# Three layer norms of a two-layer trunk kernel: tiles normalised directly, and the start and the query copies reordered

## The reference, cut to what matters

```python
for layer in range(DEPTH):                      # DEPTH = 2
    mix = _even_mixer(...) if layer % 2 == 0 else _odd_mixer(...)
    x = _layer_norm(ALPHA * x + mix, ln1_g[layer], ln1_b[layer])
    x = _layer_norm(ALPHA * x + _swiglu(x, ...), ln2_g[layer], ln2_b[layer])

def _layer_norm(x, g, b):
    mu = jnp.mean(x, -1, keepdims=True)
    xc = x - mu
    var = jnp.mean(xc * xc, -1, keepdims=True)
    return xc * lax.rsqrt(var + LN_EPS) * g + b
```

## Time and profile before

| what | value |
|---|---|
| median of 3 runs | 1243.77 us (1243.36 to 1244.42) |
| the profiled execution | 1243.55 us, its span 1241.7 us |
| PE busy | 1227.7 us, 99% of the span |
| DVE, ACT, POOL busy | 436.9, 450.6, 587.9 us |
| granted PE clock, mean | 0.998 of 2.4 GHz |
| DMA | 122.96 MB, mean 99 GB/s |

### The profile page before, as it was taken

One profiled execution on the slowest core, in us unless ns is written; L12 is line 12 of the kernel. 1 busy time (PEld: TensorE's weight loads), 2 busy tenths in 40 slices (PEclk: granted clock), 3 DMA queues, 4 the chain that ended last, 5 costly groups with the idle time before them and its releaser, 6 DMA issues.

```text
span 1241.7 us, 17153 instructions
## 1 busy us (share of the span) xinstructions
PE 1227.7 (99%) x7112; PEld 1012.4 (82%) x7112; DVE 436.9 (35%) x772; ACT 450.6 (36%) x670; POOL 587.9 (47%) x280
## 2 busy tenths in 40 slices
PE   9999999999999999999999999999999999999997
PEld 7878887888888888887777889888788888888885
DVE  4556526201011100127678845654511111110105
ACT  4167825232223221225544455542532233221211
POOL 4244444943444343445744347444684444435341
PEclk9999999999999999999999999999999999999999
DMA  9321052333322333232353342124233222324231
GB/s 321 96 69 69 3 169 69 102 102 102 99 93 80 98 124 118 102 102 60 92 123 116 91 114 94 27 69 136 68 102 102 92 92 88 102 85 146 75 102 68
DMA packets 106064, 122.96 MB, mean 99 GB/s; under 512 B 18946, under 2 KB 80580, under 8 KB 105988
## 3 DMA queue, kind: packets, MB, share of 16 engines
q1 hardware_dynamic: 98244, 118.56, 29.9%
q10 hardware_dynamic: 7744, 3.32, 1.1%
HBM read 117.93 MB, written 3.70 MB: 98 GB/s over the span
## 4 chain that ended last, share of the span: by engine, by line
PE 95%; DVE 3%; DVEq 0%; ACT 0%; issue 0%; ACTq 0%
PE bank L1665 27%; PE bank L1666 27%; PE bank L1667 27%; PE bank L2088 4%; PE bank L1696 1%; PE bank L1697 1%; PE bank L1709 1%; DVE stats L1239 1%; DVE x_tm L1237 1%; PE bank L1919 1%; PE bank L2197 1%; PE bank L1731 1%; PE bank L2034 1%; PE bank L2180 0%; PE bank L1855 0%; DVE x_tm L1200 0%
## 5 line engine op out<-in xcount | busy, mean ns | idle before, releaser
L681 POOL TENSOR_TENSOR w_lo<-w_raw,w_hi 128x1024 fp32r<-128x1024 f32 (+1 forms) x200 | 470.2, 2373 | 546.9 <-ACT w_hi L816 521.8
L1665 PE MATMUL bank<-x_hi,w_hi 128*128 128x512 f32 x880 | 344.3, 391 | 0.0
L1666 PE MATMUL bank<-x_lo,w_hi 128*128 128x512 f32 x880 | 342.5, 389 | 0.0
L1667 PE MATMUL bank<-x_hi,w_lo 128*128 128x512 f32 x880 | 342.5, 389 | 0.0
L816 ACT ACTIVATE w_hi<-w_raw 128x1024 fp32r<-128x1024 f32 (+1 forms) x200 | 196.4, 1032 | 206.5 <-issue 161.2
L1665 PEld LDWEIGHTS bank<-x_hi,w_hi 128*128 128x128 f32 x880 | 165.2, 188 | 35.4 <-issue 0.8
L1667 PEld LDWEIGHTS bank<-x_hi,w_lo 128*128 128x128 f32 x880 | 165.2, 188 | 34.4
L1666 PEld LDWEIGHTS bank<-x_lo,w_hi 128*128 128x128 f32 x880 | 165.2, 188 | 33.7
L1246 DVE TENSOR_TENSOR f_ab<-bank,f_ab 128x512 f32<-128x512 f32 x44 | 30.4, 692 | 364.7 <-PE bank L1667 364.7
L1667 PE MATMUL bank<-w_hi,h_lo 128*128 128x512 f32 x352 | 136.9, 389 | 0.0
L1665 PE MATMUL bank<-w_hi,h_hi 128*128 128x512 f32 x352 | 136.9, 389 | 0.0
(11 more groups left out here) (291 smaller groups left out, 1252.1 us busy)
## 6 DMA issues: line engine op xcount, KB each, us to landing
w_raw<-ffn_w_gate_dram SPq DMA_DIRECT2D x22, 1024.0 KB, 5.3
w_raw<-ffn_w_up_dram SPq DMA_DIRECT2D x22, 1024.0 KB, 5.3
w_raw<-ffn_w_down_dram SPq DMA_DIRECT2D x20, 1024.0 KB, 5.0
w_raw<-od_w_in_dram SPq DMA_DIRECT2D x16, 1024.0 KB, 5.8
w_raw<-ev_w_in_dram SPq DMA_DIRECT2D x8, 1024.0 KB, 5.6
w_raw<-ev_w_out_dram SPq DMA_DIRECT2D x4, 1024.0 KB, 5.1
w_raw<-od_w_out_dram SPq DMA_DIRECT2D x4, 1024.0 KB, 5.1
x_fm<-x_fm_dram SPq DMA_DIRECT2D x8, 256.0 KB, 6.9
```

Of the source, the lines that this page charges most:

```text
L681: pool.tensor_tensor(w_lo[:, b % 2, c], w_raw[:, b % 2, c], w_hi[:, b % 2, c].bitcast(F32), ALU.subtract).then_inc(w_lo_ready, 1)
L1665: pe.matmul(out_ap, st[0], mv_[0], start=start, stop=False)
L1666: pe.matmul(out_ap, st[0], mv_[1], start=False, stop=False)
L1667: return pe.matmul(out_ap, st[1], mv_[0], start=False, stop=stop)
```

## The change

Four edits in one.

In norms 1 to 3 DVE normalises each tile directly behind its own statistics. ACT rounds the first half of the next weight block ahead of the last tile's square root, and the second half behind `round_x`. With `round_x(2)` now ahead of them, the three DMAs of ACT in norm 2 are issued after it.

At the start 12 warm-up matmuls are run instead of 16; PE starts "sq" with four matmuls of high parts only, and then takes the other two products of column block 0.

ACT copies two tiles of queries and keys before it rounds the second "gv" block.

```diff
+            def split_part(b, j):
+                assert split[0] == b
+                if j == 0:
+                    act.wait_ge(w_landed[b % 2], 16 * (b // 2 + b % 2))
+                    act.wait_ge(*block_end[b - 2])
+                    low_weights_all(act, b - 2)
+                act.activation(w_hi[:, b % 2, pieces(b)[j]], w_raw[:, b % 2, pieces(b)[j]], ACT.Copy).then_inc(w_hi_ready, 1)
+                split[0] += j
+
-            def round_x(i):
+            def round_x(i, b):
...
+                split_part(b, 1)
+
-            def layer_norm(i):
+            def layer_norm(i, b=None):
                 for t in range(NT):
+                    if t == NT - 1 and b is not None:
+                        split_part(b, 0)
                     act.wait_ge(s["ln_var"], NT * (i - 1) + t + 1)
...
-            split_to(first_block[("gv",)] + 1)
             for t in range(NT):
+                if t == 2:
+                    split_to(first_block[("gv",)] + 1)
                 full(act, ("qT", t))
...
-            layer_norm(1)
-            split_to(first_block[("gate", 0, 0)] + 1)
-            round_x(1)
+            layer_norm(1, first_block[("gate", 0, 0)] + 1)
+            round_x(1, first_block[("gate", 0, 0)] + 1)
...
-            layer_norm(2)
-            split_to(first_block[("conv", KD)] + 1)
+            layer_norm(2, first_block[("conv", KD)] + 1)
+            round_x(2, first_block[("conv", KD)] + 1)
             act.dma_start(ba_w[:, :, :], ...)
...
-            round_x(2)
...
                             dve.bn_aggr(mv[:, t, :], ...).then_inc(s["ln_var"], 1)
-                            if i == 4:
-                                normalise(t)
-                            elif t:
-                                normalise(t - 1)
-                if i < 4:
-                    normalise(NT - 1)
+                            normalise(t)
...
-            for _ in range(16):
+            for _ in range(12):
                 pe.matmul(bank(("skv", NT - 1))[:, :], warm[:, 0:P], warm[:, :], start=True, stop=True)
-            tm_group(("sq",), lambda k: low_part_there(pe, 0, k))
+            pe.wait_ge(s["w_first_hi"], 1)
+            pe.wait_ge(s["x_hi_ready"], 1)
+            for t in range(NT):
+                pe.matmul(fill(("sq", t))[:, :], x_hi[:, 0, tile_cols[t]], weights(0, 0, 0, 512)[0], start=True, stop=False)
+            weights_there(0, 0)
+            low_part_there(pe, 0, 0)
+            for t in range(NT):
+                pe.matmul(bank(("sq", t))[:, :], x_lo[:, 0, tile_cols[t]], weights(0, 0, 0, 512)[0], start=False, stop=False)
+                pe.matmul(bank(("sq", t))[:, :], x_hi[:, 0, tile_cols[t]], weights(0, 0, 0, 512)[1], start=False, stop=False)
+            tm_group(("sq",), lambda k: low_part_there(pe, 0, k), begun=1)
```

More of the change, by code:

```diff
@@ L1129, in _ @@
             split_to(first_block[("gate", 1, 0)])
-            layer_norm(3)
-            split_to(first_block[("gate", 1, 0)] + 1)
-            round_x(3)
+            layer_norm(3, first_block[("gate", 1, 0)] + 1)
+            round_x(3, first_block[("gate", 1, 0)] + 1)
             ffn(1)
@@ L1734, in few_columns, with tm_group @@
                 done(ins, key)
-            def tm_group(name, wait_k, src=xcols, kt=KD, in_turn=False, tiles=range(NT), pair_last=False, late=0):
+            def tm_group(name, wait_k, src=xcols, kt=KD, in_turn=False, tiles=range(NT), pair_last=False, late=0, begun=0):
                 b = first_block[name]
@@ L1761, in tm_group @@
                                       start=False, stop=False)
-                    for kk, t in [(kk, t) for kk, t in steps if kk >= late or k0]:
+                    for kk, t in [(kk, t) for kk, t in steps if kk >= max(late, begun) or k0]:
                         if kk > waited:
```

## The result

The changed kernel takes 1250.45 us (median of 4 runs, 1250.03 to 1251.51), the kernel before 1243.78 beside it: a ratio of 1.0054, with a 95% interval of 1.0042 to 1.0067. It is slower, as forecast, but by 6.7 us instead of 4.4, and so 0.25 us above the top of the range, 1245.0 to 1250.2. The profiled execution took 1251.51 us, 7.96 more than that of before, and is where the working can be followed; it is the slowest of the four runs.

A forecast was written before the change was run, and what follows sets the result against it. PE was busy 1227.7 of 1241.7 us, so only some 14 us of idle time could be won, or time added. Norms +5.3, start and queries -0.9: 1243.55 + 4.4 + 0.22 = 1248.2 us, range 1245.0 to 1250.2.

The forecast's parts named there:

- What bounds a norm: Norms 1 to 3: DVE's chain ends last ahead of the next block, at 3.32 us a tile against PE's 2.72.
- Direct order: Norms 1 to 3: normalising each tile directly ends the last pair 1.00 us later per norm.
- The hold: First tile of norms 1 to 3: POOL's running operation holds DVE's normalising pair, 0.86 us more per norm.
- Rival B: Norms: POOL holds nothing, only the direct order's cost counts, +1.9 us, 1245.7; chance 0.18.
- rival C: Norms: DVE's period stays at or under PE's 2.72 us, so the kernel gets faster, 1240.5; chance 0.11.
- Rounding moved: Around norms 1 to 3: ACT's rounding out of the way lets DVE's copies go 0.08 us sooner at most.
- The net of all three terms: Per norm: direct order plus hold, 1.86 us, less 0.08 for the moved rounding, giving 1.78 us later.
- Start and queries: Ahead of the norms: new start -0.8 us, query wait gone -0.6, counted together as -0.9 (bounds -0.4 and -1.4).
- The late ba_w: Norm 2: this DMA, issued after the column blocks, still lands by 574.0 before PE's load at 574.8: nothing, bound +0.5.
- rival D: Norms: PE's idling ahead of the fourth tile's transposes halves its clock, 1.6 us a norm, 1253.0 in all; chance 0.08.
- a clock under 1.00 behind a norm: Changed profile: PE's granted clock below full after a norm would make the forecast wrong.

The follow-up runs named there:

- e08: Changed kernel with 14 extra PE transposes per norm and POOL's second half of the gate block delayed behind the first tile's normalising pair: 1245.74 us.
- e03: Kernel before with only the rounding of the next block moved around the norms and ACT's DMAs issued later, DVE's order as before: 1243.77 us.
- e02: Kernel before with each tile normalised directly in norms 1 to 3, nothing else: 1252.41 us.
- e04: Changed kernel with 20 extra PE transposes ahead of the eighth column block in each of norms 1 to 3: 1247.99 us.
- e06: Kernel before with only two tiles of queries and keys copied ahead of ACT's rounding: 1243.89 us.
- e01: Changed kernel with norms and rounding put back as before, leaving the new start and the query copies: 1242.96 us.
- e09: Changed kernel with PE turning column blocks 0 to 6 of three tiles, then their block 7, then the fourth tile, no extra work: 1249.9 us.
- e05: Kernel before with only the new start (12 warm-up matmuls, high parts first in "sq"): 1242.95 us.

## Why the prediction was right, and where it fell short

**What bounds a norm**: right. The last pair's end decides, by DVE's period, not by PE's.

**Direct order, 1.00 a norm**: right, 0.98 (e08). **The hold, 0.86**: right in kind, 0.75 measured. Rival B (no hold) and rival C (DVE keeps PE's pace) are out: the adds are 3.32 apart where nothing holds, and 4.06 where POOL does.

**Rounding moved, 0.08 a norm**: mis-sized. It is 0 in the old order (e03) and, at the full clock, 0.57 in the new one (e02 against e04). The prediction compared ACT with DVE as they stood in the earlier trace rows, and did not move DVE's end 0.61 forward against the last square root, as its own redrawn chain did. The net of all three terms still came out, 1.73 against 1.78, since the sum followed the DVE chain alone, and with the rounding moved that chain does decide.

**Start and queries, -0.9 together**: right as far as can be told, -1.0 in the medians, with an interval that reaches no change, and -0.55 at T0 of the profile. In parts, both inside the noise: the start -0.6 instead of -0.8, as the twelve warm-ups end at 5.9 to 6.9 in the profiles and not at 5.7; the queries nothing measurable (e06), what is won at 68.0 being given back at 96.8 through POOL, as said. The late ba_w cost nothing, as said.

**The clock, rival D at 0.08**: this is the step that failed, and it holds all of the excess. It happened in all three norms of the profiled execution, at 0.8 to 1.4 us each, where rival D had 1.6; a clock under 1.00 behind a norm was the prediction's own sign of being wrong. The sum had nothing for it, and the medians show 2.5 us (1250.45 - 1247.99), against an excess of 2.25 over the forecast. Three statements of that step were wrong.

First, the place. The idle stretch was put ahead of the fourth tile's transposes. It lies between the seventh and the eighth transpose of the first tile, because the eighth bank is the one whose add comes last. The length was nearly right, 2.5 against 2.2. Fewer transposes are done before it and 25 are left behind it, of which the last eight lie on the path. The earlier trace rows names the normalising, L1210. The wait for the bank, which the add (L1237) releases, was in the same list of the kernel before, 0.2 us long, and it is the one that grew:
```profile
PE bank L1841 <- DVE x_tm L1237: 0.6, 3, 0.2
```

Second, the argument "In the tail PE was idle 4.3 us with the full clock granted ..., so 2.2 should not do it". One row of one execution was read as a bound. The same tail in e08, windows behind PE's last matmul, which ends at 1234.68:
```profile
1234.70:1236.70 2.00, 0.00 (x0) 0.00 (x0) 1.90 (x4) 0.00 (x0) 0.00 (x0) 1.00 0.15 56
...
1237.50:1238.50 1.00, 0.00 (x0) 0.00 (x0) 0.58 (x3) 0.29 (x1) 0.00 (x0) 0.50 0.28 107
```
In windows of half a microsecond the fall comes 2.1 us after PE's stop there, 2.2 in e03, 4.3 in the kernel before and 5.2 in e02. Over the 13 profiles of this study the same code gives everything from 2.1 to 5.2 us. The earlier trace rows happened to show one of the late ones. Two of the thirteen came within 2.5 us, so a gap of that length was not safe by this measure either.

Third, it was taken for granted that a gap which ends before the fall is harmless. In the changed kernel and e02, with the same gap of 2.5 us in six norms, the clock fell in five. Those falls came 2.1 to 3.6 us after PE had stopped, and four of the five came when it was at work again, 0.1 to 1.1 us behind the restart. At 1.1 us a fall, the mean of the three in the changed kernel, five in six would make 3 x 5/6 x 1.1 = 2.8 us, near the 2.5 of the medians. This is an estimate in hindsight: no row of the kernel before had such a gap in a norm.

What stays open: what makes the clock fall in one norm and not in the next. The wait was the same 2.55 us in norm 2 of e02, where it stayed up, and in norm 1, where it fell. The number of falls differs between executions of the changed kernel: its four runs were granted 0.994 (the profiled one, with three falls), 0.995, 0.996 and 0.995 of the clock on average, where every run of e01 and e04 was granted 0.997 or 0.998.

## What to carry to other kernels

A helper engine that keeps step with PE has a period per tile; compare the two periods before anything else. A lag of one tile that looks like a needless delay may be what hides a round trip to another engine: here taking it out raised DVE's period from 2.8 to 3.3 us and cost 1 us a norm. When an edit opens a gap on PE, look for the bank that is released last, and price the gap twice: its length, and a fall of the clock behind it. The fall can come after the gap has ended, so look at the granted clock for some microseconds behind it. And a delay read off one execution is one draw, for the clock as for the start: look at the same place in several.

## What was not expected of the hardware

The time from PE's last matmul to the fall of its clock varied from 2.1 to 5.2 us over 13 executions of the same tail. The clock can fall after PE has gone back to work: 1 us behind the restart in norm 2 of the changed kernel, and behind 32 full-rate transposes in e09. The twelve warm-up matmuls took 4.94 us in the changed kernel's profile, 5.49 in those of e01 and e05, and 4.46 in those of e04 and e08, and the start of real work moves with them (6.34, 6.74, 6.19 and 5.99). The Trainium skill, "TensorE: Matmul & The Clock Gate", Part 1, says that how many matmuls run slowly at a kernel's start differs from run to run; the traces agree, with 4.46 to 5.49 us.
